# Five stages between the delta rule's scan and the second layer, written as one stage by tiles of 128 tokens

## What is computed

```python
# end of layer 0, r_h: the delta rule's outputs of both directions, summed
r_y = heads_layernorm(from_heads(r_h) + pre['bonus'], r_ln_w, r_ln_b, 8, 64e-5) * silu(pre['rz'])
y = concatenate([m_y, r_y], axis=-1) @ w_out          # 1024 x 1024
x = x + gate * y                                       # gate of layer 0
# begin of layer 1
shift, scale, gate = split(silu(c) @ mod_w + mod_b, 3)  # mod_w: 1024 x 3072, two rows of c: image and context
h = rmsnorm(x, norm_g) * (1.0 + scale) + shift
h = raster_to_column(h)                                # image tokens only: transposes the grid
```

## Time and profile before

| | us |
|---|---|
| median of 3 runs | 3025.61 (3023.84 to 3027.55) |
| the profiled execution's own time | 3031.57 |
| its span | 3029.8 |
| TensorE busy | 2666.8 (88%) |
| VectorE busy | 1277.9 (42%) |
| ScalarE busy | 843.4 (28%) |
| GpSimd busy | 117.9 (4%) |
| stages 2 to 5 of the list above, 1473.55 to 1788.74 | 315.2 |

### The profile page before, as it was taken

One profiled execution on the slowest core, in us unless ns is written; L12 is line 12 of the kernel. 1 busy time (PEld: TensorE's weight loads), 2 busy tenths in 40 slices (PEclk: granted clock), 3 DMA queues, 4 the chain that ended last, 5 costly groups with the idle time before them and its releaser, 6 DMA issues. The chain is left out here.

```text
span 3029.8 us, 47816 instructions
## 1 busy us (share of the span) xinstructions
PE 2666.8 (88%) x21060; PEld 1650.3 (54%) x21060; DVE 1277.9 (42%) x2007; ACT 843.4 (28%) x1522; POOL 117.9 (4%) x133
## 2 busy tenths in 40 slices
PE   7799999999899599899569779977977999989678
PEld 2454566666444488688434224433433867768533
DVE  3220434533576355355502232313513566656604
ACT  2111222233557255344220110101001334343301
POOL 0000000000112100000010000003000000000000
PEclk9799999999899799899879879987988999999779
DMA  6200111110556611110142530001012000010033
GB/s 242 78 28 6 57 41 47 56 47 18 146 156 147 162 59 32 64 59 32 71 188 97 213 120 28 28 13 49 28 56 90 22 22 15 1 42 1 14 153 97
DMA packets 89772, 214.00 MB, mean 71 GB/s; under 512 B 6245, under 2 KB 45285, under 8 KB 85978
## 3 DMA queue, kind: packets, MB, share of 16 engines
q1 hardware_dynamic: 79854, 173.58, 16.5%
q0 software_dynamic: 9712, 37.36, 4.8%
HBM read 155.87 MB, written 55.05 MB: 70 GB/s over the span
## 5 line engine op out<-in xcount | busy, mean ns | idle before, releaser
L689 PE MATMUL psum<-arena,m_fill_weight 128*128 128x512 f32 (+1 forms) x864 | 336.3, 530 | 5.8 <-DMA m_fill_weight<-in_l_w_in 5.8
L2353 PE MATMUL psum<-arena,g_weight 128*128 128x512 f32 (+1 forms) x512 | 219.0, 554 | 27.6 <-DMA g_weight<-in_l_w_in 27.6
L389 PE MATMUL psum<-arena,project_weight_y 128*128 128x512 f32 x512 | 221.7, 596 | 13.1 <-DMA project_weight_y<-in_l_w_in 13.1
L689 PEld LDWEIGHTS psum<-arena,m_fill_weight 128*128 128x128 f32 x864 | 157.8, 194 | 108.3 <-issue 91.8
L389 PEld LDWEIGHTS psum<-arena,project_weight_y 128*128 128x128 f32 x512 | 97.8, 191 | 137.7 <-issue 123.0
L389 PE MATMUL psum<-arena,project_weight_m 128*128 128x512 f32 (+3 forms) x432 | 158.2, 530 | 15.0 <-DMA project_weight_m<-in_l_w_in 15.0
L2599 DVE COPY_PREDICATED g_pairs<-g_masks,psum 128x512 f32<-128x512 uint8 x128 | 93.5, 730 | 142.5 <-PE psum L2381 142.5
L1166 PE MATMUL psum<-gp_weight,arena 128*128 128x512 f32 x320 | 149.9, 617 | 0.0
L2344 PE MATMUL psum<-g_weight,arena 128*128 128x128 f32 x1152 | 145.0, 275 | 0.0
L2103 PE MATMUL psum<-out_weight,arena 128*128 128x512 f32 x256 | 113.8, 607 | 29.1 <-DMA out_weight<-in_l_w_out 29.1
L2112 PE MATMUL psum<-out_weight,arena 128*128 128x512 f32 x320 | 137.7, 592 | 0.0
(11 more groups left out here) (381 smaller groups left out, 4192.3 us busy)
## 6 DMA issues: line engine op xcount, KB each, us to landing
mod_weight<-in_l_mod_w SPq DMA_DIRECT2D x16, 1536.0 KB, 7.5
arena<-scratch_operands SPq DMA_DIRECT2D x40, 512.0 KB, 4.0
scratch_operands<-arena POOLq DMA_DIRECT2D x16, 640.0 KB, 8.2
scratch_operands<-arena POOLq DMA_DIRECT2D x32, 320.0 KB, 11.2
g_weight<-in_l_w_in SPq DMA_DIRECT2D x20, 512.0 KB, 4.6
m_fill_weight<-in_l_w_in SPq DMA_DIRECT2D x18, 512.0 KB, 3.8
out_weight<-in_l_w_out SPq DMA_DIRECT2D x16, 512.0 KB, 10.9
project_weight_y<-in_l_w_in SPq DMA_DIRECT2D x4, 2048.0 KB, 8.0
```

What stands on the lines that cost most here:

```text
L389: last = nc.tensor.matmul(p.psum[0:rows, u % 8, 0:n], lhsT, rhs, start=(k == 0), stop=(k == KT - 1))
L689: last = nc.tensor.matmul(p.psum[:, FILL + f % BANKS, 0:width], weight[:, q % PIECES, k, :], hT[:, k, at:at + width], start=(k == 0), stop ...
L2353: last = nc.tensor.matmul(bank[:, 0:width], w[:, kk, :], hT[:, kk, first:first + width], start=(kk == 0), stop=(kk == KT - 1))
```

## The change

The layernorm, the turn back, the output product and the second layer's modulated norm are replaced by one stage, `stage_finish`. It goes over the ten tiles of 128 tokens with four engines at work on different tiles, and neither `r_y`'s half of `mix` nor `x1` is read back from DRAM (`x1` is still stored, for the last stage). Further:

- The shift and scale columns of layer 1's `mod_w` (8 pieces of 1 MB) are loaded by SP during the second scan, into the part of `arena` behind the scan's ring and a new tensor `next_mod_weight`.
- These products write the four groups of 512 columns to partitions 0, 32, 64 and 96 of one PSUM bank, and not to partitions 0 and 1 of one bank each. The gate's columns (two groups) come later, between tiles, with weights that GpSimd loads.
- Shift and scale are known before the first tile is turned, and the modulation is part of the copy out of PSUM: channels 0 to 511 by ScalarE, 512 to 1023 by VectorE.
- `silu` of the conditioning is kept from layer 0. `stage_modulated_norm` keeps only layer 0's form.

```diff
@@ stage_rwkv_scan, SP @@
                     sp.dma_start(window[:, s % SLOTS], operands[d, c]).then_inc(operands_loaded[s % SLOTS], 16)
+                    if d == 1 and s >= SLOTS and s - SLOTS < KT:
+                        sp.dma_start(next_weights(s - SLOTS), p.dram["l1_mod_w"].rearrange("(p k) n -> p k n", k=KT)[:, s - SLOTS, 0:2 * D]
+                                     ).then_inc(next_loaded, 16)
...
@@ stage_finish, TensorE @@
+                def turn_bonus(t):
+                    pe.wait_ge(bonus_loaded[t % SLOTS], 16 * (t // SLOTS + 1))
+                    if t:
+                        pe.wait_ge(sig["added"], t)
...
+                def last_products(t):
+                    pe.wait_ge(sig["mixed"], t + 1)
+                    products(t, range(WT, KT)).then_inc(sig["products_ready"], 1)
...
+                def shift_and_scale():
+                    for k in range(KT):
+                        for g in range(SHIFT_SCALE):
+                            last = nc.tensor.matmul(p.psum[group_rows(g), MOD, :], p.silu[:, k, :], weights(k)[:, g * BANK:(g + 1) * BANK],
+                                                    start=(k == 0), stop=(k == KT - 1))
+                    last.then_inc(sig["mod_ready"], 1)
...
+                turn_bonus(0)
+                shift_and_scale()
+                turn_bonus(1)
+                first_products(0)
+                turn_bonus(2)
+                turn_columns()
+                turn_back(0)
+                for i in range(TILES):
+                    last_products(i)
+                    if i + 1 < TILES:
+                        turn_back(i + 1)
+                    if i:
+                        turn_low(i - 1)
+                    if i + 1 < TILES:
+                        first_products(i + 1)
+                    if i:
+                        turn_high(i - 1)
+                    if i + 3 < TILES:
+                        turn_bonus(i + 3)
+                    if 1 <= i <= 4:
+                        next_gate_products(2 * i - 2)
+                        next_gate_products(2 * i - 1)
+                    if i >= 6:
+                        spread_gate(i - 6)
+                turn_low(TILES - 1)
+                turn_high(TILES - 1)
@@ stage_finish, ScalarE @@
+                square_heads(0)
+                square_heads(1)
+                shift_heads(0)
+                for i in range(TILES):
+                    if i + 2 < TILES:
+                        square_heads(i + 2)
+                    if i + 1 < TILES:
+                        shift_heads(i + 1)
+                    if i:
+                        copy_low(i - 1)
+                    square_rows(i)
+                    if i >= 6:
+                        copy_gate(i - 6)
+                copy_low(TILES - 1)
@@ stage_finish, GpSimd @@
+                multiply(0)
+                pool.wait_ge(sig["mod_ready"], 1)
+                for k in range(GATE_SLOTS):
+                    load_gate_weight(k)
+                for i in range(TILES):
+                    if i + 1 < TILES:
+                        multiply(i + 1)
+                    store(i)
...
@@ stage_finish, VectorE @@
+                norm_heads(0)
...
+                add_bias(0, SHIFT_SCALE, "rows_ready")
+                norm_heads(1)
+                dve.wait_ge(sig["columns_ready"], 1)
...
+                for i in range(TILES):
+                    if i >= 2:
+                        copy_high(i - 2)
+                    if i + 2 < TILES:
+                        norm_heads(i + 2)
+                    finish_rows(i)
...
+                copy_high(TILES - 2)
+                copy_high(TILES - 1)
@@ build_program @@
-        stage_modulated_norm(p, 0, x0, gate[0], hT)
-        first_layer(p, arena, hT, mix, p.scratch["spill"])
-        stage_output(p, 0, arena, mix, gate[0], x0, range(TILES), x1, p.x1_stored)
-
-        stage_modulated_norm(p, 1, x1, gate[1], hT)
+        stage_modulated_norm(p, x0, gate[0], hT)
+        first_layer(p, arena, hT, mix, p.scratch["spill"], gate, x0, x1)
+
```

More of the change, by code:

```diff
@@ L553 @@
 R_LEVELS = 6
+R_RING = 8
 M_IN = 5 * W + 4 * M_HEADS
@@ new lines, in _ @@
+                load_bonus(1)
+                load_mix(0)
+                for k in range(WT):
+                    load_weight(k)
+                load_factor(0)
+                load_bonus(2)
+                for k in range(WT, KT):
+                    load_weight(k)
+                sp.wait_ge(sig["mod_ready"], 1)
+                sp.dma_start(gate, gate_dram).then_inc(sig["gate_loaded"], 16)
+                load_x(0)
+                for t in range(1, SLOTS):
+                    load_mix(t)
+                    load_factor(t)
+                    load_x(t)
@@ new lines, in turn_back, with products @@
+                def turn_back(t):
+                    pe.wait_ge(sig["head_normed"], t + 1)
+                    if t:
+                        pe.wait_ge(sig["shifted"], WT * t)
+                    turned_chunks(p, y_chunks.rearrange("p c j n -> p c j n"), t, BACK).then_inc(sig["turned_back"], 1)
+                def products(t, ks):
+                    for k in ks:
+                        if t == 0:
+                            pe.wait_ge(rows_loaded[k], 16)
+                        for n in range(2):
+                            last = nc.tensor.matmul(p.psum[:, OUT + 2 * (t % 2) + n, :], mixed[:, t % SLOTS, k, :],
+                                                    weight[:, k, n * BANK:(n + 1) * BANK], start=(k == 0), stop=(k == KT - 1))
+                    return last
@@ new lines, in copy_low @@
+                def copy_low(t):
+                    act.wait_ge(sig["low_turned"], t + 1)
+                    if t == 0:
+                        act.wait_ge(sig["scale_ready"], COLUMNS)
+                    r = region(t)
+                    for k in range(WT):
+                        dst, form = on_grid(k, t)
+                        last = nc.scalar.activation(dst, form(p.psum[:, NORM, k * P:(k + 1) * P]), ACT.Identity,
+                                                    scale=scale[:, k, r:r + 1], bias=shift[:, k, r:r + 1])
+                    last.then_inc(sig["low_copied"], 1)
@@ new lines, in copy_high @@
+                def copy_high(t):
+                    dve.wait_ge(sig["high_turned"], t + 1)
+                    r = region(t)
+                    for k in range(WT):
+                        dst, form = on_grid(WT + k, t)
+                        last = nc.vector.tensor_scalar(dst, form(p.psum[:, NORM, k * P:(k + 1) * P]), scale[:, WT + k, r:r + 1],
+                                                       shift[:, WT + k, r:r + 1], ALU.mult, ALU.add)
+                    last.then_inc(sig["high_copied"], 1)
@@ L2011, in first_layer @@
+                copy_high(TILES - 2)
+                copy_high(TILES - 1)
+def first_layer(p, arena, hT, mix, spill, gate, x0, x1):
     nc = p.nc
```

301 lines of the change are left out of this document (229 added, 72 removed).

## The result

The changed kernel takes 2928.39 us (median of 4 runs, 2920.49 to 2930.02); the kernel before, run on the same chip beside it, 3026.58 us (3023.84 to 3030.24, 4 runs). The ratio is 0.9676 (0.9658 to 0.9694): 98.2 us less. The forecast was 2922, with a range from 2907 to 2953.

The account below looks back on a forecast made before the run. TensorE's own list was taken to bound the rounds: 30 us start plus 169.7 plus the tail gives 211.8 us, against 315.2, so 103.4 less: 2928.2 for a profiled execution, 2922 as median, range 2907 to 2953.

Parts of the forecast that it names:

- in line: Rival, shift, scale and gate products: column groups do not run beside each other, 25 us more, 2947; chance 14%.
- VectorE sets the round: Rival, rounds: VectorE or the handoffs make a round 20 us, nine times 2.7 more, 2946; chance 12%.
- the lower clock: Rival, whole new stage: TensorE runs at the lower clock, its 170 us double, 3092; chance 2%.
- The start: New stage, from its first DMA to the first `last_products`: 30 us, with shift and scale products at 8.3 us plus clock rise.
- the clock's rise: Shift and scale products at the stage's start: 2 us added while TensorE's clock rises.
- The microsecond that I added for a lower clock: Before the first `last_products`: 1 us added for a lower clock behind the uncovered 3 us gap.
- The rounds: From the first `last_products` to the last product's end: TensorE's list sums to 169.7 us, a round without gate 17.3.
- The 0.1 us for each switch: Rounds, changes of array shape on TensorE: some 32 switches at 0.1 us each, 3.2 us.
- VectorE's margin: Rounds: VectorE is free at 16.3 us, the product ends at 17.3; 1 us slack, 2 us more behind it.
- The tail: Behind the last product: 10.9 us of chain with the stores landing beside it, 1.2 for block end and semaphores, end at 211.8.
- SP in the scan: Second scan: eight 1 MB loads ahead of operand loads cost 0, since operands run eight chunks ahead; uncovered, 20 us.
- The rival: Second scan: the 8 MB of loads delay the scan's operands, up to 20 us, 2942; chance 3%.

Follow-up runs that it names:

- e1: The changed kernel with the 32 shift and scale products written to partitions 0 and 1 of four banks, so all in the same array columns: 2951.74 us, ratio 0.9756.
- e3: The changed kernel with four idle 128x512 products on VectorE behind each tile's heads' norm: 2930.11 us, ratio 0.9679.
- e5: The changed kernel with 14 of the 16 bonus-turning matmuls left out for each of tiles 3 to 9: 2920.66 us, ratio 0.9652.
- e7: The changed kernel with start and tail reordered, the last tile's transposes in two free banks: 2918.88 us, ratio 0.9648.
- e2: The changed kernel with the 8 MB of shift and scale weights loaded at the new stage's start, not during the second scan: 2930.97 us, ratio 0.9683.
- e8: The changed kernel with shift and scale's 8 MB loaded in 24 pieces of 0.34 MB over both scans, not eight of 1 MB in the second: 2926.87 us, ratio 0.9681.

## Why the prediction was right

The direction, the size and the bound were right, and the rivals "in line" (e1), "VectorE sets the round" (e3) and the lower clock (1.00 in the rounds) did not come about. By its own steps, each counted from the stage's first DMA at 1474.22:

| step | forecast | measured |
|---|---|---|
| first turn of the bonus ends | 5.0 | 4.9 |
| products for shift and scale | 10.5 us | 9.1 us |
| `turn_back(0)` ends | 26.1 | 24.9 |
| first `last_products` | 30 | 28.0 |
| round without gate | 17.3 us | 17.1 us |
| rounds 1 to 4 | 19 to 20 us | 18.9 us |
| end of the last product | 199.7 | 196.6 |
| tail | 12.1 us | 14.0 us |
| end of the stage | 211.8 | 210.6 |

*The start* was 2 us shorter than its steps. For four column groups I took 3.3 times, the row of the quarters; it is 3.77. At that rate 32 products take 7.3 us, so the clock's rise cost 1.8 of the 2 us that I gave it. The estimate from the Trainium skill's "TensorE: Matmul & The Clock Gate", Part 3 (2.38 for three column tiles, hence 3.2 for four), was further off. For two groups, 4 gate products take 1.82 us, 0.455 each, 1.89 times as fast where I took 1.75. The microsecond that I added for a lower clock behind GpSimd's gap was not lost in the profiled execution of after, but 1.7 us were in e5, so the term was sound and its value is a matter of the execution.

*The rounds* were right to 1%: 168.6 us from the first `last_products` to the end of the last, forecast 169.7. The addition of the earlier trace rows worked because TensorE has no wait in them. The 0.1 us for each switch was too much on average. A switch from the long products to the 64x64 turn costs 7.06 - 6.87 = 0.19 us (1594.26 to 1601.32, against 1602.89 to 1609.76 with transposes behind), once in a round like this one; the others show next to nothing. The rule of the Trainium skill ("TensorEngine Tiling (Array Packing)", Key Properties) that a change of mode drains TensorE agrees with this 0.19 us; it was not 0.3, and at the other changes of mode the trace shows no such price.

*VectorE's margin* was put at 1 us before the product and 2 behind it; VectorE waits 1.73 and 2.53 us there, and e3 showed that 2.86 us more cost nothing.

*The tail* was 1.9 us longer than forecast, and two prices in it were low. The chain up to VectorE's last copy took 12.1 us, where I had 10.9: the two groups of four transposes took 1.08 and 1.12 us, priced 0.6 each by the clock of the rounds, while the clock has fallen in the tail (0.78 in the row from 1663 to 1684, 0.50 from 1676 to 1683). And from that copy to the next stage's first DMA it took 1.87 us, where I took 1.2. I had read this from before's end of the norm stage, and there nothing is cleared. In before's trace 0.4 us lie between the meeting of the engines and the next DMA; in after it is 1.7, with a clearing of semaphores (0.76 us) and a second meeting in between, because the new stage leaves fewer than the 40 free ones that `begin_stage` asks for. That the gate's store lands beside the chain was right in after, but by 0.3 us only (e7).

*SP in the scan* is the one term that was wrong in kind. "I take 0", because operands are loaded eight chunks ahead. They were, and none was late; and yet the scan took 9.1 us more in the profiled execution, 6.5 in the mean of six. I had looked only at who waits for the queue that the loads stand in, not at what else those 16 DMA engines carry. e2 shows that the loads are the cause, e8 that 0.34 MB at a time does little harm. The rival failed in the same way: it named up to 20 us for late operands, and the loss came by another road.

What fills TensorE's "issue" gaps can be read from the single packets in the trace. TensorE's instructions come in by DMA: the queue "q8 instruction" moved 0.79 MB in 48 packets during the scan, 16 KB each. Over the whole span it has 167 packets for TensorE's 42763 instructions, so a packet holds 256 of them. Three things then fit together:

- The seven gaps stand at the border of two such blocks: they are 512 or 768 instructions apart, within one. In the six kernels with 1 MB loads, all 31 gaps of 0.5 us and more stand at these same seven instructions.
- The instruction behind each gap starts 1.27 to 1.49 us after a packet has landed (1.2 to 1.6 in the six kernels). In no kernel does a block of the second scan start less than 1.2 us behind its packet.
- Counted from the start of the block two before, the seven packets set out after 6.6 to 9.2 us in after and after 5.0 to 6.5 us in e2, where no load stands beside them.

So TensorE waits for its own instructions, which set out late behind a 1 MB load. How the load holds a packet back, the trace doesn't show. The Trainium skill ("Runtime: NRT & Kernel Launch", Instruction fetch mechanics) says that an engine's sequencer fetches blocks of 16 KiB through its own DMA queue and that this is mostly hidden. The trace agrees with the blocks. Mostly hidden holds for the scan without loads (one "issue" wait in e2's view, of 0.4 us), and not beside 1 MB loads, with 8.96 us.

The forecast of 2922 was 6.4 us below 2928.4. The 6.5 us lost in the scan are of that size; in the stage itself the shorter start and rounds and the longer tail came to 1.2 us less than forecast, and how long an execution takes outside both varies by more than that. That the 2928.2 for an execution like the profiled one came within 1.8 us of 2930.02 is luck: the 9.1 us lost in the scan and the 8.4 us that this execution was faster ahead of it cancel.

## What to carry to other kernels

- When stages with different bounds are put side by side, add up the queue of the engine that will bound the round, then check the tightest other engine piece by piece; here both sums held to 1 or 2 us.
- Products with few rows of output (2 here) belong in different column groups of the array: in the kernel before this alone gave 27.9 us, until the loads set the pace.
- "Loaded ahead, so it is free" must be asked of the DMA engines and of every stream that they carry, an engine's own instructions among them. Here pieces of 0.34 MB cost less than pieces of 1 MB in the profiles, though the medians can't tell them apart.
- When a gap at a start or an end is closed, look at once for what stands close behind it: in e7 it was the next tile's load, 3.4 us, and at the end GpSimd's store.

## What the runs showed of the hardware

- Four products of 128x512 with 2 stationary columns, each to its own quarter of the columns over all 128 rows, take 0.2275 us each, 3.77 times as fast as in line; two groups take 0.455, 1.89 times.
- 1 MB loads beside a scan of short matmuls opened gaps of 0.5 to 2.9 us in TensorE's queue, though TensorE waited for none of their data. They stood at the borders of blocks of 256 instructions, and TensorE went on 1.2 to 1.6 us after the next 16 KB packet of instructions had landed. Pieces of 0.34 MB left two waits of 0.4 us.
- A 1 MB store to DRAM landed 3.9 us after its issue when SP issued it, and after 4.1 to 5.9 us in nine kernels where GpSimd did. There GpSimd's drain behind the landing lasted 1.61 us each time. I did not try the store from SP in the new stage.
- Clearing the semaphores between two stages, with the second meeting of the engines, took the time from the first meeting to the next stage's first DMA from 0.4 to 1.7 us.
- The same gap of 3 us in TensorE's work, at the same place, left the next eight products at 7.13 us in after, e3 and e8, and was followed by a lower clock, with 8.83, 8.83 and 8.60 us for them, in e1, e5 and e2. What decides between the two I did not find out.
